# Compressed attention and block selection as one stage: before and after

## What is computed

```
s = einsum('bqghd,bngd->bghqn', qc, kc) * scale
dist = t[:, None] - cmp_end[None, :];  valid = cmp_end[None, :] <= t[:, None]
p_cmp = masked_softmax(s - sl * dist, valid) * any(valid)
o_cmp = einsum('bghqn,bngd->bqghd', p_cmp, vc)
imp = einsum('bghqn,nm->bgqm', p_cmp, a_sel)     # then forced and future blocks
_, idx = lax.top_k(imp, 8)                       # blocks of the selected branch
return gc[..., 0:1] * o_cmp + gc[..., 1:2] * o_sel + gc[..., 2:3] * o_win
```

## Time and profile before

| | us |
|---|---|
| three runs | 3396.03, 3399.29, 3399.51 (median 3399.29) |
| the profiled execution | 3396.3 |
| its span in the trace | 3394.3 |
| TensorE busy in it | 2988.0 (88%) |
| VectorE, ScalarE, GpSimd busy | 1369.5, 998.8, 556.2 |

### The profile page before, as it was taken

One profiled execution on the slowest core, in us unless ns is written; L12 is line 12 of the kernel. 1 busy time (PEld: TensorE's weight loads), 2 busy tenths in 40 slices (PEclk: granted clock), 3 DMA queues, 4 the chain that ended last, 5 costly groups with the idle time before them and its releaser, 6 DMA issues. The chain is left out here.

```text
span 3394.3 us, 37684 instructions
## 1 busy us (share of the span) xinstructions
PE 2988.0 (88%) x13210; PEld 1759.8 (52%) x13211; DVE 1369.5 (40%) x3249; ACT 998.8 (29%) x2050; POOL 556.2 (16%) x564
## 2 busy tenths in 40 slices
PE   8999999999977658989999969999699899859990
PEld 5544444444447644545665646666544355446670
DVE  3421212111214555555565648888511111152236
ACT  1100000000005524544555536666411012113332
POOL 0121100111003430131311220000121100001116
PEclk9999999999988869999999989999899999869995
DMA  3212111121142220011111020110364333625848
GB/s 119 77 60 71 68 68 56 68 71 68 56 117 78 79 86 27 6 61 34 57 41 47 7 95 1 38 38 1 131 217 141 139 124 124 272 64 204 322 166 309
DMA packets 120754, 323.41 MB, mean 95 GB/s; under 512 B 13216, under 2 KB 49696, under 8 KB 112416
## 3 DMA queue, kind: packets, MB, share of 16 engines
q1 hardware_dynamic: 100320, 247.54, 20.6%
q0 software_dynamic: 14096, 51.39, 4.5%
q10 hardware_dynamic: 6192, 22.55, 1.6%
HBM read 206.42 MB, written 115.02 MB: 95 GB/s over the span
## 5 line engine op out<-in xcount | busy, mean ns | idle before, releaser
L305 PE MATMUL p_ps<-token_sums,p_ws 128*128 128x512 f32 x768 | 340.0, 592 | 0.0
L305 PEld LDWEIGHTS p_ps<-token_sums,p_ws 128*128 128x128 f32 x768 | 145.9, 190 | 183.7 <-issue 183.7
L305 PE MATMUL p_ps<-xnT,p_w 128*128 128x512 f32 x512 | 233.0, 598 | 5.2 <-PEq L59 5.2
L1704 PE MATMUL o_ps<-o_w,o_mT 128*128 128x512 f32 x512 | 224.0, 596 | 14.0 <-DMA o_w<-in_w_out 14.0
L314 ACT ACTIVATE p_kept<-p_ps 128x512 f32<-128x512 f32 x32 | 19.1, 598 | 737.3 <-PE p_ps L305 737.3
L1054 PE MATMUL b_po<-b_probT,vsw 128*64 128x256 f32 (+1 forms) x1824 | 232.0, 376 | 0.0
L327 DVE TENSOR_TENSOR p_kept<-p_ps,p_kept 128x512 f32<-128x512 f32 x96 | 66.4, 692 | 391.5 <-PE p_ps L305 391.5
L1130 DVE CUSTOM_DVE_ANT_0 b_prob_s<-b_pq,b_sel 128x896 f32<-128x896 f32 (+5 forms) x192 | 167.8, 911 | 134.6 <-PE b_pq L1013 125.8
L1296 PE MATMUL d_pq<-d_keys,d_q 64*128 64x512 f32 (+3 forms) x640 | 185.4, 578 | 28.1 <-DVE d_seg_max L1401 15.8
L1013 PE MATMUL b_pq<-ks,b_q 64*128 64x512 f32 (+3 forms) x688 | 166.2, 542 | 40.4 <-DVE b_seg_max L1130 26.4
L1401 DVE CUSTOM_DVE_ANT_0 d_prob<-d_pq,d_bias 128x1024 f32<-128x1024 f32 (+6 forms) x192 | 168.0, 910 | 65.9 <-PE d_pq L1296 63.1
(11 more groups left out here) (278 smaller groups left out, 4766.9 us busy)
## 6 DMA issues: line engine op xcount, KB each, us to landing
projT<-p_stage SPq DMA_DIRECT2D x128, 256.0 KB, 2.3
y<-e_y ACTq DMA_DIRECT2D x43, 512.0 KB, 4.3
p_w<-in_wt SPq DMA_DIRECT2D x16, 1024.0 KB, 5.5
gates_T<-projT SPq DMA_DIRECT2D x16, 1024.0 KB, 10.0
wgu<-in_w_gu SPq DMA_DIRECT2D x4, 4096.0 KB, 15.6
y<-m_zeros POOLq DMA_DIRECT2D x20, 512.0 KB, 11.8
p_xin<-in_x SPq DMA_DIRECT2D x16, 512.0 KB, 3.7
mergedT<-m_stage SPq DMA_DIRECT2D x8, 1024.0 KB, 11.6
```

Of the source, the lines that this page charges most:

```text
L305: mm = nc.tensor.matmul(ps[n % 8][:], weights[:, k, :], moving[:, k, :], start=(k == 0), stop=(k == HK - 1))
L1704: mm = nc.tensor.matmul(ps[b][k][:], mT[:, b, dt, :], w[:, dt, k * 512:(k + 1) * 512], start=(dt == 0), stop=(dt == DT - 1))
```

## The change

The two stages become one. Its 16 steps run over (chunk c, pair i), both groups at once, in one block without a loop or barriers. The queries of all pairs and all constants are loaded in `compress`, behind `kw`.

- Chunk c uses only the first 32(c+1) compressed keys in scores, additions, exponentials and products (`width`). The transposes keep 128 columns.
- The queries are divided by slope at the projection: ScalarE multiplies the stored tiles of the first two `j` by `qscale` in place, and SyncE waits for that. So the score plus the plain distance needs no bias for each head; the slope is a constant of the exponential. `scale_queries` and its waits are gone from the sparse stage.
- VectorE per step: `maxima` (one addition out of PSUM over both groups and four tiles, one maximum, one small instruction), and `gate` (one sum, reciprocal, weight, one product). Chunk 0 has two more small ones.
- GpSimd per step: rate times probability, and for i > 0 an addition into `pbar`; VectorE's weighted copy goes into `gated` instead.
- Values come out turned: `vc` is the stationary operand, 512 tokens move, and the result (64 rows per group) goes straight to DRAM as `ycT` (16 stores of 256 KB). The sparse stage loads it into `y` (32 loads of 128 KB); its "C" flats, 32 of 520, are gone, and `add_up` waits for the load.
- The selection of chunk c follows three steps (transposes at step 4c+5, product at 4c+6, choice at 4c+7) inside the same stage.

```
-        with nc.Fori(0, PAIRS) as i:
-            with nc.Block() as block:
...
+        def width(n):
+            return 32 * (steps[n][0] + 1)
...
+            def add_up(n):
...
+                pool.wait_ge(rate_ready, n + 1)
+                if i == 0:
...
+                    nc.gpsimd.tensor_tensor(acc, prob[n % 4][:, :, :, 0:w], rate, ALU.mult).then_inc(summed, 1)
+                else:
+                    pool.wait_ge(summed, n)
+                    nc.gpsimd.tensor_tensor(plain[:, :, :, 0:w], prob[n % 4][:, :, :, 0:w], rate, ALU.mult).then_inc(plain_ready, 1)
+                    pool.wait_ge(plain_ready, n - c)
+                    nc.gpsimd.tensor_tensor(acc, acc, plain[:, :, :, 0:w], ALU.add).then_inc(summed, 1)
...
+            for n in range(LAST):
+                if n + 2 < NS:
+                    scores(n + 2)
+                if n < NS:
+                    pe.wait_ge(gate_done, n + 1)
+                    turn(gated[n % 2], step_use[n])
+                if 1 <= n <= NS:
+                    values(n - 1)
...
+                if n < NS:
+                    copy(probT[:, n % 2], step_use[n], values_at[n - 2] if n >= 2 else 0)
+                if 1 <= n <= NS:
+                    evict(n - 1)
...
+                if n + 2 < NS:
+                    exponentials(n + 2)
...
+            def maxima(n):
...
+                nc.vector.tensor_tensor(x, pq[n % 2][:, :, :, 0:w], away, ALU.add).then_inc(added, 1)
+                dve.wait_ge(added, n + 1)
+                nc.vector.tensor_reduce(stat[:, n % 4, 0], x, AX.X, ALU.max).then_inc(maxed, 1)
...
+            def gate(n):
...
+                link(nc.vector.tensor_reduce(total, x, AX.X, ALU.add))
...
+                    nc.vector.reciprocal(rate, total).then_inc(rate_ready, 1)
+                dve.wait_ge(rate_ready, n + 1)
+                link(nc.vector.tensor_tensor(weight, rate, by, ALU.mult))
+                if n >= 2:
+                    dve.wait_ge(turned, step_use[n - 2] + 1)
+                nc.vector.tensor_tensor(gated[n % 2][:, :, :, 0:w], x, weight.unsqueeze(3).to_broadcast([P, GROUPS, 4, w]), ALU.mult).then_inc(gate_done, 1)
...
+            for n in range(LAST):
+                if n < NS:
+                    gate(n)
+                if n + 2 < NS:
+                    maxima(n + 2)
+                if n in sel_choice:
+                    choose(sel_choice[n])
...
-        flats += [(u, "W", 2 * p + 1, (1,)), (u, "R", 0, (0, 1)), (u, "C", 0, (0, 1))]
+        flats += [(u, "W", 2 * p + 1, (1,)), (u, "R", 0, (0, 1))]
```

More of the change, by code:

```diff
@@ L309, in _ @@
         def _(act):
-            for q in range(NQ):
+            act.wait_ge(qscale_in, 16)
+            for q, (j, c) in enumerate(quads):
                 act.wait_ge(made, 7 * q + 1)
@@ L674, in _ @@
             sp.dma_start(s.b_wdist[:], d["win_dist"]).then_inc(s.b_const_in, 16)
-            sp.wait_ge(ya_out, 16)
+            for n, (c, i) in enumerate(steps):
+                sp.wait_ge(evicted, n + 1)
+                sp.dma_start(d["ycT"][i][:, c * 512:(c + 1) * 512], y[:, n % 2, :]).then_inc(stored[n % 2], 16)
+            for b in range(2):
+                sp.wait_ge(stored[b], 16 * NS // 2)
         @block.gpsimd
         def _(pool):
-            pool.wait_ge(s.b_const_in, 32)
-            for k in range(2):
-                scale_queries(nc, pool, s, k)
+            for x in gated + pbar:
+                nc.gpsimd.memset(x[:], 0.0).then_inc(cleared, 1)
@@ L702, in _, with scores @@
-            importance(len(steps) - 1)
+            def scores(n):
+                c, i = steps[n]
+                w = width(n)
+                if i == 0:
+                    pe.wait_ge(s.q_in[c], 16)
+                if n >= 2:
+                    pe.wait_ge(added, n - 1)
+                for j in range(4):
+                    t = (4 * c + j) * P
+                    for g in range(GROUPS):
+                        rows = slice(g * HD, (g + 1) * HD)
+                        mm = nc.tensor.matmul(pq[n % 2][:, g, j, 0:w], s.q[rows, i, t:t + P], s.kc[rows, 0:w], start=True, stop=True)
+                mm.then_inc(scored, 1)
@@ new lines, in turn, with values @@
+            def turn(x, use):
+                if use >= 1:
+                    pe.wait_ge(copied, use)
+                for g in range(GROUPS):
+                    for j in range(4):
+                        mm = nc.tensor.transpose(pt[g][:, j, :], x[:, g, j, :], s.ident[:])
+                mm.then_inc(turned, 1)
+            def values(n):
+                pe.wait_ge(copied, step_use[n] + 1)
+                if n >= 1:
+                    pe.wait_ge(evicted, n)
+                for g in range(GROUPS):
+                    mm = nc.tensor.matmul(po[g * HD:(g + 1) * HD, :], s.vc[:, g * HD:(g + 1) * HD], probT[:, n % 2, g, :], start=True, stop=True)
+                mm.then_inc(valued, 1)
@@ new lines, in importance @@
+            def importance(c):
+                pe.wait_ge(copied, sum_use[c] + 1)
+                if c >= 1:
+                    pe.wait_ge(weighed, c)
+                for g in range(GROUPS):
+                    for j in range(4):
+                        mm = nc.tensor.matmul(pi[:, g, j, :], sumT[:, g, j * P:(j + 1) * P], s.overlap[:], start=True, stop=True)
+                mm.then_inc(valued, 1)
+            pe.wait_ge(s.cmp_const_in, 80)
+            scores(0)
+            scores(1)
+            for n in range(LAST):
[6 more added lines that the diff above has]
+                    values(n - 1)
+                if n in sel_turn:
+                    c = sel_turn[n]
+                    pe.wait_ge(summed, PAIRS * c + PAIRS)
+                    turn(pbar[c % 2], sum_use[c])
+                if n in sel_product:
+                    importance(sel_product[n])
@@ L737 @@
+            dve.wait_ge(s.cmp_const_in, 80)
+            maxima(0)
+            maxima(1)
+            dve.wait_ge(cleared, 2)
+            for n in range(LAST):
+                if n < NS:
+                    gate(n)
[3 more added lines that the diff above has]
+                    choose(sel_choice[n])
 SELW = 20 * P
```

443 lines of the change are left out of this document (178 added, 265 removed).

## The result

The changed kernel takes 3314.5 us (median of 4 runs, 3311.5 to 3315.8) against 3399.4: ratio 0.9749, 95% interval 0.9732 to 0.9766, or 85 us less. The forecast was 3336 and its range began at 3314. Its profiled execution took 3311.51 us, with a span of 3309.4.

What follows compares the result with a forecast made beforehand. No engine bounds the old 170.8 us stretch throughout; TensorE bounds the sparse stage. New stage 121.8 (-49) and sparse stage -12 give 3396.3 - 61 = 3335, adjusted to 3336 for the median; range 3314 to 3364.

Steps and rivals of the forecast that it cites:

- rival A: New stage: gated goes before GpSimd's product, so GpSimd waits at no cost; 20 us less, 3316; chance 0.12.
- start to the first `gated`: New stage's head: two steps of scores at low clock, first maxima, exponentials and gate in a row; 9 us.
- chunk 1: New stage's second chunk: four steps bound by VectorE, 4.4 us each, product wait included.
- the choices: Two block choices inside VectorE's list in the new stage, 3.3 us each, 6.6 together.
- B: New stage: clock stays 0.50 well beyond chunk 0, GpSimd's addition also meets VectorE's small instructions; 3364; chance 0.20.
- C: New stage: the two-step lead fails and steps run serially; stage 217 us, time 3430; chance 0.04.
- The lock: New stage: GpSimd's product holds VectorE's gated for its whole length, one product a step; 20 us.
- Chunk 0 and the clock: New stage's first chunk: TensorE-bound steps of 3.9 us; three at low clock take 7.1 each, 10 us more.
- Chunk 3: New stage's last chunk: four steps bound by VectorE, 7.4 us each, product wait included.
- The end: Behind the last gated: transposes, values, sums and product 8, last choice 3.3, clearing and barrier 2.4; 13.7 us.
- The sparse stage: Removing 32 C transposes (9.9 us) and GpSimd's scalings (3.6) gives 13.5, of which 12 us taken.
- Rival D: Sparse stage gives nothing back, its gaps absorb the C flats; 3348; chance 0.62 together with the forecast.

Runs made afterwards that it cites:

- e5_no_sums: GpSimd works on one column of each tile instead of the whole width, against the changed kernel (sums wrong); 3300.3 us, one run.
- e2_c_back: 32 C flats put back as idle work (two transposes, ScalarE's copy of 256 columns) in the changed kernel; 3338.3 us.
- e1: GpSimd's first mask additions wait until VectorE has done its four of pair 0, against the changed kernel; 3304.0 us.
- e6: GpSimd's product waits for the maxima two steps ahead, its addition for the next gated, against the changed kernel; 3311.3 us.

## Why the prediction was right, and where its sizes were off

The time, 3314.5, lies half a microsecond above the range's lower end, 21.5 below the forecast and nearest to rival A's 3316, though A did not happen. That it lies inside is partly luck: nearly every term below was too long, and only the tail was clearly too short. The mechanism of the new stage held: a lock on `gated`, VectorE as the bound, and a lead that kept the steps from running in series. By the forecast's own terms (us; measured by the ends of `gated` in the changed kernel):

| term | forecast | measured |
|---|---|---|
| start to the first `gated` | 9 | 6.8 |
| chunk 0, three periods, and low clock | 11.7 + 10 | 11.8 |
| chunk 1 | 17.6 | 17.3 |
| chunk 2, with one choice | 23.6 + 3.3 | 27.0 |
| chunk 3, with one choice | 29.6 + 3.3 | 27.9 |
| end | 13.7 | 19.9 |
| stage | 121.8 | 110.8 |
| sparse stage | -12 | -25.8 |

**Right.** The totals of chunks 1 and 2 within 2% (a period of chunk 1 was 4.0 against 4.4, and 5.2 in the one step whose `maxima` is already chunk 2's); the choices (3.4 each). GpSimd's products at 0.61, 1.04, 1.47 and 1.90 us, and `gated` held by them: rival A, the other order, did not happen. Neither did B, a heavier stage, nor C, serial steps. One sign named for B did show: the clock was at 0.50 beyond chunk 0, around 1090, 1114 and 1140. In the steps this cost next to nothing (VectorE waited 0.25 us for scores behind the first of them, and not at all behind the second), in the tail it did. VectorE is the bound in chunk 3. The loads landed in time, and no instruction waited for the load of the compressed output. The projection and `compress` cost 0.5.

**The lock, 20 us forecast; `gated` was 13.7 over its own times, and 8.7 came back without GpSimd's work.** I charged the whole product; `gated` starts 0.16 us behind the product and waits for what is left of it, 0.31, 0.74, 1.17 and 1.59 us in the four chunks, and in the last step not at all. The weight and the gap before `gated` already ran beside the product. The other way round is in the trace too: at 1133.85 VectorE's `gated` came first and GpSimd's product took 2.90 us instead of 1.90.

**Chunk 0 and the clock, 10 us forecast, 2.3 measured.** The clock did fall, as the earlier trace rows suggested. Windows of the changed kernel (us; busy PE, PEld, DVE, ACT, POOL; clock, DMA share, GB/s):

```profile
1044.00:1047.00 3.00, 2.43 (x44) 2.46 (x45) 1.23 (x5) 1.54 (x3) 2.62 (x3) 1.00 0.49 161
1047.00:1050.00 3.00, 0.49 (x8) 0.35 (x6) 1.84 (x8) 3.00 (x15) 1.01 (x3) 0.54 0.97 270
...
1053.00:1056.00 3.00, 3.00 (x22) 2.94 (x23) 1.91 (x6) 2.71 (x10) 1.32 (x2) 0.50 1.02 429
...
1059.00:1062.00 3.00, 3.00 (x32) 1.96 (x28) 2.58 (x8) 3.00 (x11) 0.16 (x1) 1.00 0.97 402
...
1090.00:1093.00 3.00, 3.00 (x12) 1.55 (x10) 2.86 (x6) 1.08 (x2) 0.14 (x1) 0.50 0.00 0
...
1114.00:1117.00 3.00, 0.00 (x0) 0.00 (x0) 2.90 (x4) 0.00 (x0) 1.90 (x1) 0.50 0.00 0
...
1135.00:1146.00 11.00, 10.21 (x38) 6.62 (x38) 3.80 (x27) 2.47 (x5) 4.10 (x2) 0.50 0.14 49
```

But the scores of three steps had run at full clock at once (48 records in 2.92 us at 1044.57), which also made the start shorter than my 9. VectorE then waited twice for scores made at the low clock, 0.99 and 1.35 us, and `gated` of steps 1, 2 and 3 ended 2.9, 4.0 and 4.9 us after the one before; I had put three steps at 7.1. I priced an operation at the low clock and took it for the path, though a lead of two steps lay between. Nor is TensorE the bound of chunk 0 at full clock: a step takes it 3.1 to 3.3 us (scores 1.0 to 1.1, transposes 1.09, values 1.08), not the 3.9 that I made of the earlier trace rows (scores 2.1, values 0.7), and VectorE's own 2.9 to 3.6 (the periods less its waits) is as long. That the three periods of 11.8 meet my 11.7 is therefore chance.

**Chunk 3, 5 us too much.** The last two steps have no `maxima` behind them; I gave the last one a whole period (7.4) where it takes 3.5.

**The end, 6.2 us too little.** TensorE's timeline in the tail of the changed kernel:

```profile
1134.48 3.62 PE L604 MATMUL a_pi<-overlap,a_sumT 128*128 128x32 f32 x16
1137.91 1.95 PE L587 MATMUL a_pt<-ident,a_gated 128*128 128x128 f32 x8
1139.79 1.98 PE L595 MATMUL a_po<-a_probT,vc 128*64 128x512 f32 x4
1142.56 1.97 PE L595 MATMUL a_po<-a_probT,vc 128*64 128x512 f32 x4 [0.79 <-ACT a_y L656]
1144.46 1.94 PE L587 MATMUL a_pt<-ident,a_pbar 128*128 128x128 f32 x8
1147.57 1.97 PE L604 MATMUL a_pi<-overlap,a_sumT 128*128 128x32 f32 x16 [1.18 <-ACT a_sumT L649]
```

The last `gated` was ready at 1134.99, but its transposes stood behind chunk 2's importance product until 1137.91 (2.9 us). And until 1146 all of it ran at 0.50: that product took 3.62 us instead of the 1.97 of the last one, which ran at full clock again, and the four transposes and values took 7.84 us where the same instructions take 1.06 to 1.09 each at full clock, 3.5 more. In `e5_no_sums`, whose tail had the full clock from 1129 on, the stretch from the last `gated` to the end of the stage was 14.3 us instead of 19.9: near my 13.7. So, by this comparison, the low clock explains 5.6 of the 6.2 us. The forecast had it at the stage's head; most of its cost came at the tail, where nothing runs ahead.

**The sparse stage, 12 forecast, 25.8 measured.** This is the largest mistake. The step that failed is the sum "0.31 us, 32 times 9.9", taken from L1035's start to the next product's: a distance between two starts is not the price of a piece with a bank, a copy and a place in the rotation. Putting the pieces back gave 20.9 to 23.5 us, with `e2_c_back`, which is nearest to the old pieces, 21.8. The scalings were worth 2.6 at the mask of the earlier trace rows, where I had 3.6. That leaves about 1.4 of the 25.8 without a cause. Rival D, no gain there, is out. The masks at the start stayed as forecast (14.5 us), and `e1` shows that they need not have.

## What to carry to other kernels

Where TensorE is 95% busy, price a removed piece of its rotation by putting idle ones back, not by its matmuls' distance: here 0.65 to 0.7 us against 0.31. Where VectorE and GpSimd both work on operands in SBUF, give GpSimd its long instructions beside VectorE's reductions and additions out of PSUM, and never beside a run of small instructions that others wait for: one wait was worth 10 us. And price a low clock by what covers it: behind a lead of two steps it cost 2.3 us here, in the tail, where nothing runs ahead, about 5.6.

## What the runs showed of the hardware beyond this

The clock fell in this stage when VectorE's choice had kept TensorE without work. Windows of the changed kernel around the first choice inside the steps:

```profile
1084.00:1087.00 3.00, 0.00 (x0) 0.00 (x0) 2.93 (x23) 1.36 (x6) 0.00 (x0) 1.00 0.23 87
1087.00:1090.00 3.00, 0.31 (x2) 0.32 (x3) 2.90 (x5) 0.00 (x0) 1.47 (x1) 0.70 0.00 0
```

After them come the 0.50 of 1090 to 1093 above, and the same again at 1114. Nor is the clock the same in all runs. These windows of `e2_c_back`, whose stage has the same instructions as the changed kernel's, show it return some 6 us later (0.75 in 1062 to 1065; in the changed kernel it was back by 1059). Behind that point `gated` of step 5 is 2.5 us later than in the changed kernel and stays so: the difference between the stages of 110.8 and 113.4 us in the table:

```profile
1059.00:1062.00 3.00, 3.00 (x20) 2.57 (x18) 1.69 (x4) 1.62 (x8) 0.00 (x0) 0.50 0.95 385
1062.00:1065.00 3.00, 3.00 (x23) 1.49 (x23) 1.74 (x7) 2.23 (x6) 1.40 (x2) 0.75 0.13 46
```

The sparse stages of 760.8 and 763.9 us (`e6`) part in the same way. Ten microseconds of it, from about 60 us behind its start, in the changed kernel and then in `e6_pool_shift`:

```profile
1214.90:1224.90 10.00, 8.40 (x50) 4.33 (x50) 6.30 (x15) 5.10 (x6) 0.00 (x0) 1.00 0.01 2
```

```profile
1210.40:1220.40 10.00, 10.00 (x37) 5.35 (x37) 3.90 (x8) 2.93 (x4) 0.00 (x0) 0.51 0.01 2
```

Differences of 3 us between kernels that share the stretch are therefore not to be read as effects of an edit elsewhere.
